# A hybrid decoder trunk on one core: gates by tanh, statistics over more steps, one convolution tile on GpSimd, prologue and tail in another order

## The chip, the core and the metric

The kernel runs on one core of a Trainium2 chip. The time is the device time of one execution, in microseconds, of a single program that holds the whole computation. PE is TensorE, ACT is ScalarE, DVE is VectorE, POOL is GpSimd, SP is SyncE, which here only issues DMAs. Each engine has its own instruction queue and works it off in order; engines wait for each other by semaphores.

## The reference

Two layers over 512 tokens of width 1024, in float32. Each layer:

```python
h = h + 0.5 * swiglu(rms(h), ffn1_wi, ffn1_wo)             # width 2816
n = rms(h);  z = n @ w_in                                  # conv, sgu, q, kv, 24 head gates, 3 x 1024 gates
y_a = silu(layer_norm(causal_depthwise_conv31(a * sigmoid(g)) + bias)) @ conv_out
y_b = (u * (tril(ws) @ v + b)) @ sgu_out                   # u, v = gelu(z_sgu), v normed, chunks of 128
y_c = nsa(rms(q), kv, sigmoid(z_ngate)) @ nsa_out          # compressed, selected and window attention, 8 heads
g_a, g_b, g_c = split(sigmoid(z_merge), 3)
h = h + (g_a * y_a + g_b * y_b + g_c * y_c) @ w_out
h = h + cross_attention(rms(h), rms(mem))                  # 4 heads, 256 memory tokens
h = h + 0.5 * swiglu(rms(h), ffn2_wi, ffn2_wo)
```

With 512 tokens, all eight blocks of 64 are selected, so the selected and the window attention have the same mask.

## The kernel before

**Weights.** Activations lie transposed, features on partitions and 512 tokens in the free dimension. Every product is made of *units*: a tile of up to 1024 x 128 weights against 512 tokens. For precision, weight and activation are split in a high and a low part and three products are added (high x high, high x low, low x high; PE, lines 600, 603, 606), so a unit of 8 row blocks is 24 matmuls and one of 4 is 12. A unit's path: SP loads it into one of two `raw` slots (`unit`, it waits for the low half of the unit two before); ACT copies it to `wH` (`split`, line 1110, called three units ahead by `ahead`); POOL subtracts to `wL` (`low`, line 569); PE multiplies into one of four PSUM banks `pg`; DVE takes the result out (`evac`).

**The attention stage.** Four pairs of heads times four query tiles give 16 steps s; step s has `COLS[s % 4] + 1` key tiles (4, 1, 3 and 2 of them). Before it lies the opening: the units of the last two query pairs (`U_QP2`) and the first two gates, with the spatial gating's transposes and products dropped between their matmuls (`opening`, one piece every four matmuls). Then for i = 1 to 16 PE runs `branch(i - 1)` (12 matmuls) and `gate(i + 1)` (24), with a piece of `attention(i, p)` after every second matmul: p = 0, 3, 6, ... transposes a group of step i-1's probabilities into the one bank `pT` (`turned`, line 651), p = 1 and 7 compute the scores of step i (line 808), p = 5, 8, ... multiply by the values (line 860). ACT's queue in step i is: `split`, `turned_out(i-1, 0)`, `exps(i, 0)`, `turned_out(i-1, 1)`, `split`, `turned_out(i-1, 2)`, `exps(i, 1)`, the other `turned_out`, `weighted(i)`, `merge_gate(i)` (line 1248). DVE's is `maxes(i, 0)` (line 1787), evacuation of the gate unit, `maxes(i, 1)`, of the branch unit, `weigh(i)` (lines 1800, 1805). `exps` waits for `maxes`, `weigh` for `exps`, `weighted` for `weigh`, the next `turned` for `weighted`.

**What lies beside it on DVE.** The convolution: 4 tiles of 31 taps (`conv(count)`, line 1631), done in portions from the conv units on; up to two running tiles are held in PSUM, in the attention all are in SBUF. `conv(count)` takes taps in turn from the first two unfinished tiles. Its LayerNorm needs a mean and a variance, summed over partitions by PE with a matrix of ones (`middle`, line 867). Query pairs are normalised by `squares`, `stat` on PE, `root` on ACT (line 1153) and a reciprocal on DVE (`normed`, lines 1494 and 1607). The order of the groups and statistics that pass `pT` is the list `order`, and each has its place in it (`STEP`).

**The rest.** The prologue loads x, transposes it on PE, loads 19 small parameter arrays and four of convolution weights, transposes them and copies them to `pall`; each layer copies its part to `par` (line 1587). `norm` makes high and low parts of the scaled input (lines 1110 and 1501). The two layers are passes of one loop on every engine. In the cross-attention, `xo_part(k)` (lines 1069 to 1071) accumulates four output units head by head beside the chain of the last head.

## Time and profile before

| | us |
|---|---|
| median of 3 runs | 2892.61 (2889.74 to 2893.19) |
| the profiled execution's own time | 2888.34 |
| its span | 2886.6 |
| PE busy | 2735.6 (95%) |
| DVE, ACT, POOL busy | 1210.4, 1194.8, 1149.1 |
| mean granted clock of TensorE | 0.974 |

The profile gives, for each engine, busy time, groups of instructions by line and shape, what ended each idle time, and the share of full speed that TensorE's clock was granted. Lines are those of the kernel before; line 1110 is the copy that all ACT copies go through. Weight loads (PEld) overlap PE.

### The profile page before, as it was taken

To read this page: it belongs to the slowest core of one execution; us is meant where nothing else is said; L and a number is where in the kernel's file an instruction comes from. 1 tells how busy PE (TensorE), PEld (TensorE's weight loads), DVE (VectorE), ACT (ScalarE), POOL (GpSimd) and SP (SyncE) were. 2 spreads that over 40 slices of the span, in tenths; PEclk is the share of its full clock that TensorE was granted. 3 is DMA by queue.
4 is the path that set the end of the run, shared out by engine and by line. 5 is a ranking of instruction groups with operands and counts; after the bars stand their busy time and mean duration, and the time that the engine had idled before them with its cause. 6 is when DMAs were issued, how large, how long until landed. Compare 5 with 4: busy or idle time off the path is not lost.

```text
span 2886.6 us, 39881 instructions
## 1 busy us (share of the span) xinstructions
PE 2735.6 (95%) x13132; PEld 2155.3 (75%) x13132; DVE 1210.4 (42%) x1860; ACT 1194.8 (41%) x1758; POOL 1149.1 (40%) x502
## 2 busy tenths in 40 slices
PE   6999999987999989999999999999889999899999
PEld 5888888754567867888878888886556687688887
DVE  4222267677334444121241212776863354431212
ACT  4322343455774454222252223334566644542321
POOL 3443453322325514444444444433223363244443
PEclk8999999988999999999999999999889999999999
DMA  3335333211114313333333352422112242133332
GB/s 103 105 95 124 103 103 81 66 45 41 45 48 117 106 41 102 95 96 101 88 89 102 95 132 87 106 74 59 44 34 56 70 115 83 52 102 95 96 101 80
DMA packets 493309, 243.61 MB, mean 84 GB/s; under 512 B 49656, under 2 KB 491362, under 8 KB 493154
## 3 DMA queue, kind: packets, MB, share of 16 engines
q1 hardware_dynamic: 493154, 241.62, 30.1%
q8 instruction: 88, 1.44, 0.2%
q14 instruction: 67, 0.55, 0.1%
HBM read 239.46 MB, written 2.10 MB: 84 GB/s over the span
## 4 chain that ended last, share of the span: by engine, by line
issue 61%; POOL 26%; PE 12%; POOLq 1%; DVE 0%; DVEq 0%
POOL wL L569 26%; PE pg L600 4%; PE pg L606 4%; PE pg L603 4%; POOLq L568 1%; POOLq L574 1%; DVE big L2050 0%; DVE xT L1538 0%; PE pg L651 0%; DVEq L72 0%; POOL tab L553 0%; POOL tab L535 0%; POOL sacc L534 0%; POOLq L561 0%; POOL tabc L555 0%
## 5 line engine op out<-in xcount | busy, mean ns | idle before, releaser
L569 POOL TENSOR_TENSOR wL<-raw,wH 128x1024 fp32r<-128x1024 f32 (+1 forms) x480 | 1144.8, 2386 | 1714.5 <-ACT wH L1110 1714.4
L600 PE MATMUL pg<-gxH,wH 128*128 128x512 f32 (+1 forms) x2448 | 974.8, 398 | 32.3 <-DVE gxL L1501 25.8
L606 PE MATMUL pg<-gxH,wL 128*128 128x512 f32 (+1 forms) x2448 | 956.9, 391 | 0.0
L603 PE MATMUL pg<-gxL,wH 128*128 128x512 f32 (+1 forms) x2448 | 953.0, 389 | 0.0
L1110 ACT ACTIVATE wH<-raw 128x1024 fp32r<-128x1024 f32 (+1 forms) x480 | 475.5, 991 | 564.7 <-PE pg L606 376.5
L600 PEld LDWEIGHTS pg<-gxH,wH 128*128 128x128 f32 x2448 | 466.1, 190 | 150.0 <-issue 33.7
L603 PEld LDWEIGHTS pg<-gxL,wH 128*128 128x128 f32 x2448 | 466.0, 190 | 105.5 <-issue 20.1
L606 PEld LDWEIGHTS pg<-gxH,wL 128*128 128x128 f32 x2448 | 466.5, 191 | 92.1 <-issue 3.0
L606 PE MATMUL pg<-hH,wL 128*128 128x512 f32 x1024 | 410.9, 401 | 0.0
L600 PE MATMUL pg<-hH,wH 128*128 128x512 f32 x1024 | 406.9, 397 | 3.7 <-POOL wL L569 3.7
L603 PE MATMUL pg<-hL,wH 128*128 128x512 f32 x1024 | 406.1, 397 | 0.0
L1538 DVE SCALAR_TENSOR_TENSOR xT<-pg,xT 128x512 f32<-128x512 f32 x128 | 88.4, 691 | 421.3 <-PE pg L606 419.2
L603 PEld LDWEIGHTS pg<-hL,wH 128*128 128x128 f32 x1024 | 194.4, 190 | 53.2 <-issue 13.3
L600 PEld LDWEIGHTS pg<-hH,wH 128*128 128x128 f32 x1024 | 194.9, 190 | 44.9 <-POOL wL L569 4.5
L606 PEld LDWEIGHTS pg<-hH,wL 128*128 128x128 f32 x1024 | 195.2, 191 | 38.0 <-issue 1.0
L1110 ACT ACTIVATE hH<-tmp 128x512 f32 x88 | 55.6, 632 | 302.5 <-DVE tmp L1553 302.5
L1553 DVE TENSOR_TENSOR tmp<-pg,tmp 128x512 f32<-128x512 f32 x88 | 60.9, 692 | 255.1 <-PE pg L606 252.7
L1548 DVE TENSOR_TENSOR tb<-pg,rstd 128x512 f32<-128x512 f32 x88 | 60.8, 690 | 246.6 <-PE pg L606 245.2
L1164 ACT ACTIVATE tmp<-tb 128x512 f32<-128x512 f32 x88 | 55.6, 632 | 258.5 <-DVE tb L1548 258.4
L1263 ACT ACTIVATE prob<-prob,nb 128x512 f32<-128x512 f32 (+3 forms) x128 | 70.9, 554 | 106.1 <-DVE nb L1790 105.8
L1631 DVE SCALAR_TENSOR_TENSOR convb<-convb,par 128x512 f32<-128x512 f32 x110 | 110.4, 1028 | 4.4
L651 PE MATMUL pA<-ident,prob 128*128 128x128 f32 x416 | 66.5, 287 | 46.0 <-ACT sq L1110 32.6
(218 smaller groups left out, 2085.9 us busy)
## 6 DMA issues: line engine op xcount, KB each, us to landing
raw<-in_ffn_wi SPq DMA_DIRECT2D x352, 256.0 KB, 3.1
raw<-in_w_in SPq DMA_DIRECT2D x200, 256.0 KB, 3.2
raw<-in_ffn_wo SPq DMA_DIRECT2D x128, 256.0 KB, 3.0
raw<-in_ffn_wo SPq DMA_DIRECT2D x64, 192.0 KB, 2.6
raw<-in_xkv SPq DMA_DIRECT2D x32, 256.0 KB, 3.1
raw<-in_w_out SPq DMA_DIRECT2D x32, 256.0 KB, 3.1
raw<-in_sgu_out SPq DMA_DIRECT2D x32, 128.0 KB, 2.2
raw<-in_conv_out SPq DMA_DIRECT2D x32, 128.0 KB, 2.2
```

The source lines that it names most:

```text
L569: pool.tensor_tensor(wL[:, s % 4, 0:n, :], raw[:, s % 2, 0:n, :], wH[:, s % 4, 0:n, :].bitcast(F32), ALU.subtract)\
L600: mm(o, wH[:, s, k, :], rh(k), start=(k == 0), stop=False)
L603: mm(o, wH[:, s, k, :], rl(k), start=False, stop=False)
L606: last = mm(o, wL[:, s, k, :], rh(k), start=False, stop=(k == kt - 1))
L651: return pe.transpose(dst, src, ident[0:k, 0:k])
L1110: return act.activation(o, i, ACT.Copy, **kw)
L1164: act.activation(sil, tb[:, 0, :], ACT.Silu).then_inc(silu, 1)
L1263: act.activation(t, t, ACT.Exp, bias=nb[:, s % 2, b, e:e + 1], scale=-1.0, accum_out=dn[:, s % 2, b, e:e + 1])
L1538: STT(xT[:, k, :], bank, by, xT[:, k, :], ALU.mult, ALU.add).then_inc(evac, 1)
L1548: TTt(tb[:, 0, :], bank, rstd[:, :], ALU.mult).then_inc(evac, 1)
L1553: TTt(hb, bank, sr, ALU.mult).then_inc(evac, 1)
L1631: STT(to, cin[:, j, k:k + T], w, o, ALU.mult, ALU.add)
```

## The change

Sigmoids of gates are written as (1 + tanh(x/2)) / 2: the merge gates' half goes into the residual's factor of W_out (0.5 for 1.0), the branch product becomes (tanh + 1) x bank in one instruction, and the head gates are scaled when they are copied. The convolution's own sigmoid stays. The roots of query pairs 2 and 3 move from the opening into steps 2 and 3, through `pT`; the mean from step 6 to step 5; the variance stays in step 7. Convolution tile 0 goes to POOL, one tap behind each `low` from U_KV + 2 on and two from U_QP2 on; DVE waits for it (`conv_in`) ahead of the mean's sum. DVE's portions in the attention become 3 in step 2, 3 and 3 in step 3 and all the rest at the end of step 4. The high and low copies of the convolution's output are spread over step 8. Two of the memory's low halves come before the last branch. `xo_part` covers three units, and its first part comes before the last head's norms and scores. In the prologue ACT issues 19 parameter loads, and the third weight split follows the first norm's high halves, which wait only for their own residual; the next layer's `par` is copied ahead of the second FFN.

```diff
@@ the order of turned groups and statistics
+EXTRA = {2: "q2", 3: "q3", 5: "mean"}
-if i == 6:
-    order.append("mean")
+if i in EXTRA:
+    order.append(EXTRA[i])
@@ SP: the loads of gains and norms (11 + 8 DMAs) leave; act.dma_start issues them ahead of act.wait_ge(consts, 1)
-for g, at in ((norm_ffn1, G_F1), (norm_mix, G_MIX), (norm_xattn, G_X),
...
-        sp.dma_start(ctab[at:at + n, 0:L, cols], g).then_inc(pro_par, 16)
@@ GpSimd
             low(l, first + s, i)
 with pool.Fori(0, L) as l:
-    lows(l, 0, U_XKV)
+    lows(l, 0, U_KV)
+    k, o, term = 0, cacc[:, CT, :], wsn[:, :, :].rearrange("p g t -> p (g t)")
+    for u in range(U_KV, U_XKV):
+        if u == U_KV + 2:
+            pool.wait_ge(cin_in, risen(cin_in, l, 1))
+        low(l, u)
+        for _ in range(0 if u < U_KV + 2 else 1 if u < U_QP2 else 2):
+            if k == CONV_W:
+                break
+            w = col(P_CW + CT * CONV_W + k)
+            if k == 0:
+                pool.tensor_scalar(o, cin[:, CT, 0:T], w, col(P_CB + CT), ALU.mult,
+                                   ALU.add)
+            else:
+                pool.tensor_scalar(term, cin[:, CT, k:k + T], w, 0.0, ALU.mult,
+                                   ALU.add)
+                pool.drain()
+                pool.tensor_tensor(o, o, term, ALU.add)
+            pool.drain()
+            k += 1
+            if k == CONV_W:
+                pool.drain().then_inc(conv_in, 1)
+    assert k == CONV_W
     lows(l, U_XKV, U_XO)
     for u in range(U_XO, U_F2):
@@ PE: middle, opening, attention
         pe.wait_ge(stat_in, risen(stat_in, l, s))
-        mm(bank[:, :], ones[:, :], sacc[:, :], start=True, stop=True).then_inc(st_mm, 1)
+        weights = bdon if key in ("q2", "q3") else ones
+        mm(bank[:, :], weights[:, :], sacc[:, :], start=True, stop=True)\
+            .then_inc(st_mm, 1)
...
             v_turned((0, 3, 6, 10).index(p))
-        if p in (5, 9, 14, 16):
-            mixed((5, 9, 14, 16).index(p))
+        if p in (5, 9, 12, 15):
+            mixed((5, 9, 12, 15).index(p))
         if p == 1:
...
             scores((0, 0))
-        if p == 11:
-            pe.wait_ge(sg_out, risen(sg_out, l, 2))
-            stat(l, 8, bdon)
         if p == 13:
             scores((0, 1))
-        if p == 19:
-            pe.wait_ge(sg_out, risen(sg_out, l, TT))
-            stat(l, 9, bdon)
     def attention(i, p):
-                middle("mean", 10)
+            elif i in EXTRA and a == n:
+                middle(EXTRA[i], {"q2": 8, "q3": 9, "mean": 10}[EXTRA[i]])
         elif p % 3 == 1:
@@ PE: cross-attention
-        for m in range(4):
+        for m in range(3):
...
+    xo_part(0)
     x_norms(3)
     x_scores(3)
-    xo_part(0)
     x_turned(2, 0)
...
     xo_part(3)
-    for m in range(4, 8):
+    for m in range(3, 8):
@@ ACT: norm and the start of a layer
     def high(k):
-        act.wait_ge(evac, risen(evac, l, 0 if u0 is None else u0 + k + 1))
+        act.wait_ge(evac, risen(evac, l, k + 1 - KD if u0 is None else u0 + k + 1))
         copy(dst(k), xT[:, k, :], scale=col(gain + k)).then_inc(gx_h, 1)
...
             high(k)
+        split(l, 2)
     for k in range(KD):
         if u0 is not None:
...
+    split(l, 0)
+    split(l, 1)
     made[0] = 3
     act.wait_ge(par_in, risen(par_in, l, 1))
     norm(l, 0, G_F1, gx_tile, None)
@@ ACT: gates
     act.wait_ge(ng_in, risen(ng_in, l, 1))
-    act.activation(hb, sr, ACT.Sigmoid).then_inc(ng_sig, 1)
+    act.activation(hb, sr, ACT.Tanh, scale=0.5).then_inc(ng_sig, 1)
...
         act.wait_ge(evac, risen(evac, l, gate_unit(n) + 1))
-        act.activation(t, t, ACT.Sigmoid).then_inc(mg_sig, 1)
+        act.activation(t, t, ACT.Tanh, scale=0.5).then_inc(mg_sig, 1)
@@ ACT: opening and steps
+    def conv_high(k):
+        copy(hH[:, BR["A"] + k, :], cacc[:, k, :]).then_inc(br_h, 1)
     ahead(l, U_QP2)
...
     v_out(3)
-    root(l, 8, rv, 1.0 / DH)
     ahead(l, gate_unit(0))
...
     weighted(0)
-    root(l, 9, rv, 1.0 / DH)
     merge_gate(0)
...
         turned_out(i - 1, 0)
+        if i == 8:
+            conv_high(0)
         if i < NS:
...
         turned_out(i - 1, 1)
-        if i == 6:
-            act.wait_ge(st_mm, risen(st_mm, l, STEP["mean"] + 1))
-            copy(sil, pT, scale=-1.0 / DC).then_inc(st_out, 1)
+        if i == 8:
+            conv_high(1)
         ahead(l, gate_unit(i + 1))
...
             exps(i, 1)
+        if i == 8:
+            conv_high(2)
         for g in range(3, n):
             turned_out(i - 1, g)
+        if i in (2, 3):
+            act.wait_ge(st_mm, risen(st_mm, l, STEP[EXTRA[i]] + 1))
+            act.activation(rv[:, :], pT, ACT.Sqrt, bias=eps[:, 0:1],
+                           scale=1.0 / DH).then_inc(st_out, 1)
+        if i == 5:
+            act.wait_ge(st_mm, risen(st_mm, l, STEP["mean"] + 1))
+            copy(sil, pT, scale=-1.0 / DC).then_inc(st_out, 1)
         if i < NS:
             weighted(i)
         merge_gate(i)
             act.drain()
-            for k in range(KB):
-                copy(hH[:, BR["A"] + k, :], cacc[:, k, :]).then_inc(br_h, 1)
+        if i == 8:
+            conv_high(3)
     def merged_high(m):
@@ DVE: parameters
-with dve.Fori(0, L) as l:
-    dve.tensor_copy(par[:, :], pall[:, bass.ds(l, 1), :]
+def par_of(n):
+    dve.tensor_copy(par[:, :], pall[:, bass.ds(n, 1), :]
                     .rearrange("p a c -> p (a c)")).then_inc(par_in, 1)
...
        ALU.mult)
+dve.memset(pall[:, L, :], 0.0)
+dve.drain()
+par_of(0)
+dve.drain().then_inc(evac, risen(evac, 0, 0))
+dve.sem_inc(sq_used, risen(sq_used, 0, 0))
+with dve.Fori(0, L) as l:
     norm(l, 0, gx_high, gx_low, G_F1, None)
     root_of(l, 0, rstd)
@@ DVE: taps, branches
         TTt(cin[:, j, CONV_W - 1:TP], tb[:, 0, :], sil, ALU.mult)
-        dve.drain()
-        inputs.append(j)
+        if j == CT:
+            dve.drain().then_inc(cin_in, 1)
+        else:
+            dve.drain()
+            inputs.append(j)
     dve.memset(cin[:, :, 0:CONV_W - 1], 0.0)
     for j in range(4):
...
         dve.wait_ge(mg_sig, risen(mg_sig, l, n + 1))
+        t = mrg[:, m, :] if n < 8 else (hb, sr)[n % 2]
+        bank = ready(l, u)
+        STT(t, tb[:, n % 2, :], 1.0, bank, ALU.add, ALU.mult).then_inc(evac, 1)
         if n < 8:
-            scaled(mrg[:, m, :], l, u, by=tb[:, n % 2, :])
             return
-        t = (hb, sr)[n % 2]
-        scaled(t, l, u, by=tb[:, n % 2, :])
         dve.drain()
         last = TTt(mrg[:, m, :], mrg[:, m, :], t, ALU.add)
@@ DVE: opening and steps
     dve.wait_ge(ng_tr, risen(ng_tr, l, 1))
-    dve.tensor_copy(gates[:, :, :], pT[:, :].rearrange("p (a c) -> p a c", a=4)
-                    [:, :, 0:NG])
+    TS(gates[:, :, :], pT[:, :].rearrange("p (a c) -> p a c", a=4)[:, :, 0:NG], 0.5,
+       0.5, ALU.mult, ALU.add)
     dve.drain()
...
     scaled(qT[:, 2, :], l, U_QP2)
-    squares(qT[:, 2, :])
     maxes(0, 0)
     mixed(1)
-    normed(l, 8, qT[:, 2, :], g8[:, 2:3])
-    dve.drain().then_inc(q_ok, 1)
     scaled(qT[:, 3, :], l, U_QP2 + 1)
-    squares(qT[:, 3, :])
+    mixed(2)
     maxes(0, 1)
-    mixed(2)
     mixed(3)
...
     weigh_c(0)
-    normed(l, 9, qT[:, 3, :], g8[:, 3:4])
-    dve.drain().then_inc(q_ok, 1)
-    conv(4)
+    def late_pair(j):
+        dve.wait_ge(st_out, risen(st_out, l, STEP[f"q{j}"] + 1))
+        dve.reciprocal(rv[:, :], rv[:, :])
+        dve.drain()
+        STT(qT[:, j, :], qT[:, j, :], g8[:, j:j + 1], rv[:, :], ALU.mult, ALU.mult)
+        dve.drain().then_inc(q_ok, 1)
     for i in range(1, NS + 1):
...
         gate(i)
-        if i < 6:
-            conv(5)
+        if i in (2, 3):
+            conv(3)
         if i == 7:
...
         if i == 8:
-            low("A", 4)
+            low("A", 4, (0,))
         if i < NS:
             maxes(i, 1)
+        if i == 8:
+            low("A", 4, (1,))
         branch(i - 1)
+        if i == 8:
+            low("A", 4, (2,))
         if i < NS:
...
                 maxes_c(i // TT + 1)
-        if i < 5:
-            conv(5)
-        if i == 5:
+        if i == 8:
+            low("A", 4, (3,))
+        if i == 1:
+            squares(qT[:, 2, :])
+        if i == 2:
+            late_pair(2)
+            squares(qT[:, 3, :])
+        if i == 3:
+            late_pair(3)
+            conv(3)
+        if i == 4:
             conv(KB * CONV_W)
+            dve.wait_ge(conv_in, risen(conv_in, l, 1))
             TTt(sacc[:, :], cacc[:, 0, :], cacc[:, 1, :], ALU.add)
...
             stat_given(None)
-        if i == 6:
+        if i == 5:
             dve.wait_ge(st_out, risen(st_out, l, STEP["mean"] + 1))
             for k in range(KB):
                 TTt(cacc[:, k, :], cacc[:, k, :], sil, ALU.add)
             dve.drain()
+        if i == 6:
             for k in range(KB):
                 TTt(sacc[:, :] if k == 0 else hb, cacc[:, k, :], cacc[:, k, :],
@@ DVE: end of the branches, residual of W_out, second FFN
             gate(NS + 1 + m)
+        if m == 7:
+            memory_low(0)
+            memory_low(1)
         branch(NS + m)
         if m == 4:
...
             last.then_inc(mem_sc, 1)
-    for i in range(4):
+    for i in range(2, 4):
...
     norm(l, 2, lambda k: xnorm_tile(hH, gxH, k), lambda k: xnorm_tile(hL, gxL, k), G_X,
-         residual(l, U_WO, 1.0))
+         residual(l, U_WO, 0.5))
...
     norm(l, 3, gx_high, gx_low, G_F2, residual(l, U_XO, 1.0))
     root_of(l, 15, rstd)
+    par_of(l + 1)
     ffn(l, U_F2, 1, None)
     dve.drain()
```

## Rows read from the trace of the kernel before

**Rows 1.** Page, part 1: busy time, share of the span, instructions of each engine.
```profile
PE 2735.6 (95%) x13132; PEld 2155.3 (75%) x13132; DVE 1210.4 (42%) x1860; ACT 1194.8 (41%) x1758; POOL 1149.1 (40%) x502
```

**Rows 2.** Waits of PE, whole span: who ended them, us in total, times, longest.
```profile
PE pA L651 <- ACT sq L1110: 45.1, 32, 5.0
...
PE pg L600 <- DVE gxL L1930: 5.6, 2, 2.8
```

**Rows 3.** Stretches of layer 0's attention: length, busy of each engine, clock, DMA.
```profile
551.00:598.20 47.20, 37.95 (x189) 27.89 (x187) 31.54 (x44) 26.88 (x40) 11.88 (x5) 0.96 0.19 51
598.20:619.00 20.80, 15.38 (x83) 9.81 (x84) 18.28 (x30) 10.19 (x23) 5.07 (x2) 0.75 0.15 39
619.00:672.30 53.30, 46.61 (x252) 29.80 (x253) 43.81 (x81) 33.21 (x64) 14.75 (x6) 0.97 0.17 45
672.30:688.10 15.80, 13.69 (x87) 8.61 (x86) 14.36 (x24) 10.82 (x24) 5.19 (x2) 1.00 0.18 52
688.10:709.00 20.90, 17.51 (x64) 10.33 (x64) 12.87 (x26) 10.96 (x20) 4.78 (x2) 0.76 0.15 38
709.00:732.90 23.90, 18.93 (x102) 11.97 (x100) 15.59 (x28) 12.71 (x24) 5.68 (x2) 0.86 0.13 34
732.90:755.40 22.50, 18.90 (x94) 11.87 (x93) 7.72 (x22) 18.54 (x32) 4.89 (x2) 0.92 0.13 35
755.40:875.00 119.60, 114.40 (x646) 75.19 (x645) 37.98 (x121) 82.17 (x158) 38.76 (x17) 0.99 0.20 54
```

**Rows 4.** Groups by line and shape: count, busy us, mean ns, idle before them.
```profile
L1248 ACT ACT_TABLE_LOAD x34 | 43.6, 1283 | 0.6
...
L1631 DVE SCALAR_TENSOR_TENSOR convb<-convb,par 128x512 f32<-128x512 f32 x110 | 110.4, 1028 | 4.4
...
L569 POOL TENSOR_TENSOR wL<-raw,wH 128x512 fp32r<-128x512 f32 x16 | 21.6, 1348 | 119.8 <-ACT wH L1110 119.8
L553 POOL TENSOR_SCALAR_AFFINE_SELECT tab<-tab 128x512 f32<-128x512 f32 x1 | 0.6, 612 | 0.0
```

**Rows 5.** Timeline of DVE and POOL, end of step 5: start, length, instruction.
```profile
683.56 5.71 DVE L1631 SCALAR_TENSOR_TENSOR convb<-convb,par 128x512 f32<-128x512 f32 x7
689.35 2.71 DVE L1899 TENSOR_TENSOR sacc<-convb 128x512 f32<-128x512 f32 x1
...
689.10 2.41 POOL L569 TENSOR_TENSOR wL<-raw,wH 128x1024 fp32r<-128x1024 f32 x1 [8.25 <-ACT wH L1110]
```

**Rows 6.** Timeline of DVE, PE and ACT, from step 4 to step 5.
```profile
667.56 0.16 DVE L1805 TENSOR_TENSOR wv<-wv,gates 128x4 f32<-128x4 f32 x1
...
674.50 0.65 PE L651 MATMUL pA<-ident,prob 128*128 128x128 f32 x4 [1.46 <-ACT sq L1110]
675.76 0.40 ACT L1263 ACTIVATE prob<-prob,nb 128x128 f32<-128x128 f32 x1
...
676.85 0.60 ACT L1110 ACTIVATE sq<-pA 128x512 f32<-128x512 f32 x1 [0.22 <-PE pA L860]
```

**Rows 7.** Timeline of POOL in the key/value units, one of seven like it.
```profile
442.26 2.40 POOL L569 TENSOR_TENSOR wL<-raw,wH 128x1024 fp32r<-128x1024 f32 x1 [3.05 <-ACT wH L1110]
```

**Rows 8.** Timeline of PE in the prologue.
```profile
8.63 6.23 PE L651 MATMUL pg<-ident,big 128*128 128x128 f32 x32 [8.63 <-DMA big<-in_x]
...
18.05 1.09 PE L651 MATMUL pA<-ident,convb 126*128 126x126 f32 x4 [3.19 <-DMA convb<-in_conv_w]
...
32.50 0.79 PE L600 MATMUL pg<-gxH,wH 128*128 128x512 f32 x1 [13.36 <-DVE gxL L1501]
```

**Rows 9.** Timeline of DVE and PE between the layers.
```profile
1453.93 0.54 DVE L1587 COPY par<-pall 128x250 f32 x1 [3.11 <-issue]
...
1456.14 0.80 PE L600 MATMUL pg<-gxH,wH 128*128 128x512 f32 x1 [6.05 <-DVE gxL L1501]
```

**Rows 10.** Timeline of PE in layer 0's cross-attention.
```profile
1045.08 3.46 PE L1019 MATMUL pA<-kT,qT 128*128 128x256 f32 x8 [3.11 <-ACTq L1428]
...
1071.70 0.57 PE L600 MATMUL pg<-hH,wH 128*128 128x512 f32 x1 [1.84 <-POOL wL L569]
```

More of the change, by code:

```diff
@@ L247, in mm_index @@
         def mm_index(n):
-            return n if n < 10 else {12: 10, 13: 11, 15: 12}[n]
+            return n if n < 8 else {12: 8, 13: 9, 15: 10}[n]
         rises = {}
@@ L272, in trunk @@
         stat_in = sig("stat_in", NSTAT - 1)
-        stat_mm = sig("stat_mm", 13)
-        stat_rt = sig("stat_rt", 13)
+        stat_mm = sig("stat_mm", 11)
+        stat_rt = sig("stat_rt", 11)
         silu = sig("silu", 2 * FT)
@@ L292, in trunk @@
         conv_sig = sig("conv_sig", 4)
+        cin_in = sig("cin_in", 1)
+        conv_in = sig("conv_in", 1)
         gelu = sig("gelu", 8)
@@ L354, in trunk @@
         BR = {"B": 4, "A": 0, "C": 4}
+        CT = 0
         BRANCH = (1, 0, 2)
@@ L911, in attention @@
                             turned(i - 1, g)
-                        elif i == 6 and a == n:
-                            middle("mean", 10)
+                        elif i in EXTRA and a == n:
+                            middle(EXTRA[i], {"q2": 8, "q3": 9, "mean": 10}[EXTRA[i]])
                     elif p % 3 == 1:
@@ L1177, in ffn @@
                     u += KD
+            for g, at in ((norm_ffn1, G_F1), (norm_mix, G_MIX), (norm_xattn, G_X),
+                          (mem_norm, G_MEM), (norm_ffn2, G_F2), (conv_b, P_CB),
+                          (conv_ln_g, P_LG), (conv_ln_b, P_LB), (sgu_norm, P_SG),
+                          (xq_norm, P_XQ), (xk_norm, P_XK)):
+                n = g.shape[1] // P
+                act.dma_start(ctab[at:at + n, 0:L, :], g.rearrange("l (a b) -> a l b", b=P))\
+                  .then_inc(pro_par, 16)
+            for half in range(2):
+                cols = slice(half * DH, (half + 1) * DH)
+                for g, at in ((nsa_q_norm.rearrange("l (a c) -> a l c", a=1), P_NQ),
+                              (nsa_k_norm.rearrange("l a c -> a l c"), P_NK),
+                              (cmp_pe.rearrange("l i a c -> i a l c")[0], P_PE),
+                              (cmp_pe.rearrange("l i a c -> i a l c")[1], P_PE + CMP_LEN)):
+                    n = g.shape[0]
+                    act.dma_start(ctab[at:at + n, 0:L, cols], g).then_inc(pro_par, 16)
             act.wait_ge(consts, 1)
             with act.Fori(0, L) as l:
-                for u in range(3):
-                    split(l, u)
+                split(l, 0)
+                split(l, 1)
                 made[0] = 3
@@ L1822, in branch, with low @@
                         last.then_inc(m_in, 1)
-                def low(name, first):
+                def low(name, first, part=range(KB)):
                     src = uG if name == "B" else cacc
-                    for k in range(KB):
+                    for k in part:
                         dve.wait_ge(br_h, risen(br_h, l, first + k + 1))
```

22 lines of the change are left out of this document (2 added, 20 removed).

## The prediction, made blind

> **What bounds the kernel now.** The page comes first: PE is busy 95% of the span, no other engine above 42% [rows 1]. An edit gains only what it takes from PE's 151 us of idle time, or from stretches in which PE works at a lowered clock. The waits of PE say whose idle time it is [rows 2]: 45.1 us end with an ACT copy of transposed probabilities, 5.6 with the memory's low halves; the rest is single waits, shown below. Then the stretches: I cut the attention of layer 0 at the gate activations of its steps [rows 3]. Opening and 16 steps take 324 us, of which PE idles 40.6: 9.3 in the opening, 5.4 in step 1, 6.7 in steps 2 to 4, 2.1, 3.4, 5.0 and 3.6 in steps 5 to 8, 5.2 in steps 9 to 16. In the same rows the granted clock is below 1: length times what is missing from 1 gives 20 us, some 18 of them with PE at work (the levels are 2.4 and 1.2 GHz, and the low rows are those with long stalls). So 59 us per layer are to be had. DVE is busy 31.5 of 47.2 and 18.3 of 20.8 us at the start, 38.0 of 119.6 at the end: the early steps wait for DVE and its convolution taps, the late ones for ACT.
>
> **Table loads (tanh).** Exponentials and sigmoids alternate: a load of 1283 ns stands before 34 of the 48 gates [rows 4]. Following the functions through the code I count 39 loads per layer from `exps_c(0)` to the memory's root; 10 stay (roots of q2, q3, var and memory, the Silu, each with its return). 29 x 1.283 = 37 us less for ACT per layer. ACT is no bound; it counts where it ends PE's idle time. A step loses two loads, 2.57 us, more than PE idles in most of steps 9 to 16 (5.2 us in eight steps): I leave 0.8. In step 8 four high copies are spread as well: 3.6 becomes 0.3. No row shows Tanh; that it stands beside Exp without a load is my assumption, as Copy does beside both; bounds are 0 and 2 loads per step (rival 3). The Trainium skill (ScalarE: Activation LUTs, "Table sets: the hidden batching unit") lists tanh in the exponential's set, and in the sigmoid's too; by the first the sum is as I take it, by the second it is rival 3.
>
> **Convolution taps.** I walked the taps through the code. Before: 68 ahead of the attention, 56 in it (4, then 5 and 5 per step, 12 in step 5, then three additions). After, tile 0 is GpSimd's; DVE does 60 ahead and 33 in it: none in step 1, 3 in step 2, 6 in step 3, and **24 at one go at the end of step 4**, the three additions behind them. At 1028 ns in the mean [rows 4] DVE loses 23 x 1.03 = 24 us per layer. In line, seven take 5.71, 0.816 each. An addition that began at 689.35 ended only 0.55 after GpSimd's operation of 2.41 us had: it was held 2.2 us [rows 5].
> *The block.* DVE's weights of step 4 are done at 667.7 [rows 6]. From there 24 x 0.816 = 19.6, two holds 4.4, additions 2.3 and another hold: 27.5 us, with bounds of 22 without holds and 33 with five, in which DVE serves nobody. Queued behind is `maxes(5, 0)`; ACT's in-order queue has `exps(5, 0)` before `turned_out(4, 1)`, and PE's third group of transpositions in step 5 needs that. PE starts the second group at 674.50; without the load before the gate it is 673.3; two pieces later, at 676, it stands. After the block come the maxima (0.6) and what is 1.7 from the exponentials' start to the copy's end [rows 6], say 2.5: 667.7 + 27.5 + 2.5 = 697.7. Stall 21.7; I take 22 in place of 2.1 (bounds 15 and 28).
> *The rest of the spreading.* Step 1 has no taps and no root ahead of its gate: 5.4 becomes 1.5. Steps 2 and 3 get a root with its load on ACT ahead of `weighted`, for which PE's next group waits, and a reciprocal on DVE behind `weigh`, for which the next maxima wait, but fewer taps: 6.7 becomes 7.2. The opening loses both reciprocals and roots (9.3 becomes 4) and gains GpSimd's taps beside it (7). Step 6: the mean was asked for a step earlier, 3.4 becomes 0.5. Step 7: four additions leave the work ahead of `var`, 5.0 becomes 2. Sum: 7 + 1.5 + 7.2 + 22 + 0.5 + 2 + 0.3 + 0.8 = 41.3 against 40.6: **idle time in the attention stays the same.**
> *Clock.* 18 us of slow work in stretches 1, 2, 3 and 5 to 8 of [rows 3]. After: one long stall, whose slow time lies mostly inside it (3.5 of work), a short one in step 7, two or three before: 9.4. Gain 8.6. **Net 8 per layer**, bounds -6 and +16.
>
> **GpSimd's tile.** 31 taps, each a tensor_scalar and a tensor_tensor of 128x512 with drains. The second kind is 1348 ns; the first is not in the trace: its bounds are the select of the same size (612) and again 1348 [rows 4]. It reads one tensor, as the select: I take 0.8, and with two drains 2.4 a tap (2.1 to 3.2). Its cover: 16 taps stand one behind each low half, where GpSimd idles 3.05 between operations of 2.40 [rows 7]; from 3.0 up PE's three units of lead absorb it. 15 come two per unit: 2.4 + 1.35 + 4 x 2.4 = 13.4 us per gate-and-branch pair, against steps of 15 or more. They end in step 2 or 3, so DVE's new wait for them at the end of step 4, with the additions queued behind it, costs nothing; it would from a tap of 5. The other price is DVE's: an operation with two SBUF inputs can be held by a tap's parts, 0.7 on average; 3 us in the opening, 2 in steps 1 and 2, both in the numbers above. The Trainium skill (GPSIMD Engine Reference, "8. Key points") speaks against this edit: DVE is about twice as fast elementwise, and the two contend when DVE has two SBUF inputs. The trace agrees on the second with its held addition of 2.71 us.
>
> **Prologue.** PE's x transposes end at 14.9, but the parameters' wait to 18.05 for 23 small loads, and the first product starts at 32.50 after 13.36 idle [rows 8], since the weights' loads follow all of them and ACT splits three units first. Now ACT issues 19 of the loads, the weights follow x and four loads on SP, and the third split comes after the high halves. Parameters turned by 16.0, four copies at 0.54 or less 2, then the 2.2 that copy, high and low half take from 1453.93 to 1456.14 [rows 9]: 20.3. **Gain 12** (9 to 13).
> **Between the layers** PE idles 6.05 [rows 9]. High halves can now run under the last residuals, and the parameter copy moved ahead of the FFN (1 us on DVE there, beside four filled banks). But DVE shows 3.11 of "issue" before its first operation of the pass: that stays. Of the 2.2 the copy and the high half go: **1.4** (0.5 to 5).
> **Cross-attention.** PE waits 3.11 for exponentials and later 1.84 for a weight [rows 10]. Nine products (PE's pace is 5.45 us a unit of 24 [rows 7], so 2.05) now fill the first wait; head 3's chain starts earlier as `xo_part(0)` is out of its middle; the fourth unit covers the weight. DVE's last norm starts as much earlier. **5.5 per layer** (2 to 7).
> **Memory.** The 5.6 us are 2.8 per layer; two low halves before the last branch take them away, and some slow time: **3 per layer** (2 to 4). (1 + tanh) x bank and the factor 0.5 replace operations of the same size: 0.
>
> **Sum.** 2 x 8 + 12 + 1.4 + 2 x 5.5 + 2 x 3 = 46. The profiled execution took 2888.3 (span 2886.6); the three runs 2889.7 to 2893.2, so I add 2: 2888.3 - 46 + 2 = **2844**. Own range 2820 to 2878.
>
> **Rivals.** (1) *The block is hidden*: the stall is 8, 14 us per layer less, 2816. For it: before, 7 taps and the additions, 10 us in step 5, cost only 3.4 in step 6. Against: this block is near three times as long, behind in-order queues. Chance 0.16.
> (2) *Slower: DVE held by GpSimd.* From the key/value units to step 2 DVE issues some 35 operations with two SBUF inputs per layer (squares, normalising products, mixes, low halves, weights). If each is held for 1.35, DVE gets 47 us more; what passes its idle time lands on PE. It decides at 23 us per layer, where it eats the gain; at 35 it gives 2890 + 2 x 12 = 2914. For it: the held addition. Against: DVE idles 15.7 us in the opening alone [rows 3]. Chance 0.12.
> (3) *Tanh still switches*: 8 us idle and 2 of slow work per layer come back, 2864. Chance 0.05.
> (4) Nothing measurable: the stall at 28 and the small parts at their low ends, 2889. Chance 0.07. The forecast has 0.60.
> A difference of 0.2% (6 us) is about what a measurement can tell from none. Faster 0.60 + 0.16 + 0.05 and a part of (4), 0.83; same 0.06; slower 0.11. The range 2805 to 2890 leaves out rival 2 and the far end of rival 1.
>
> **What would show it.** Right: few loads before gates; 22 to 24 taps in a row on DVE and, in step 5, a PE stall of 15 to 28 us that ends with an ACT copy, twice; first product near 20.5; `var`'s wait near 2. Wrong: no such stall (1); DVE operations of 1.5 to 2.7 us all over the opening and PE waiting for DVE before step 4 (2); a load before each gate (3); DVE waiting for GpSimd at the end of step 4 (a tap above 5).

## The result, and the profile after

The change makes the kernel faster by a little under 1%: 2865.37 us (median of 4 runs, 2862.85 to 2866.07) against 2891.18 for the kernel before on the same chip (2889.66 to 2893.19), ratio 0.9915, 95% interval 0.9903 to 0.9928. The medians are 26 us apart; the forecast had 46. The profiled execution took 2862.85 (span 2861.1).

The page's line of busy times and the waits of PE, of the kernel after (waited for: us in total, times, longest us):

```profile
PE 2710.0 (95%) x13132; PEld 2138.5 (75%) x13132; DVE 1167.4 (41%) x1802; ACT 1115.8 (39%) x1700; POOL 1229.9 (43%) x624
...
PE pA L663 <- ACT sq L1115: 66.5, 18, 18.3
PE pg L612 <- DVE gxL L1533: 18.7, 7, 6.3
PE pA L663 <- ACT prob L1115: 12.2, 12, 2.3
PE pA L877 <- DVEq L1521: 9.6, 2, 4.8
PE pA L627 <- DVEq L1521: 9.2, 6, 2.5
...
PE pg L612 <- POOL wL L558: 4.4, 6, 1.7
...
PE pg L612 <- DVE gxL L1984: 2.3, 2, 1.1
```

The table loads before merge gates and before the exponentials, of the kernel after:

```profile
L1269 ACT ACT_TABLE_LOAD x6 | 7.7, 1283 | 0.1
...
L1284 ACT ACT_TABLE_LOAD x2 | 2.6, 1283 | 0.0
```

Against [rows 1, 2]: PE's busy time fell by 25.6 us with the same 13132 matmuls; its idle time is 151 us in both kernels. The mean granted clock rose from 0.974 to 0.979. An estimate from these (span times what is missing from 1, 75 us before and 60 after) gives 15 us; what the other 10 are is open. The wait for ACT's copies of probabilities has grown from 45.1 to 66.5 us, and two of its 18 pieces, one in each layer, are 18.3 and 18.2 us long.

The stretches of layer 0's attention, cut as in [rows 3] (length; busy us and instructions of PE, weight loads, DVE, ACT, POOL; granted clock, DMA share, GB/s):

```profile
544.30:585.70 41.40, 35.43 (x183) 27.37 (x182) 26.38 (x38) 19.08 (x33) 37.71 (x29) 0.92 0.22 58
585.70:598.30 12.60, 11.86 (x79) 7.96 (x78) 4.56 (x17) 7.58 (x21) 8.85 (x7) 1.00 0.25 65
598.30:653.10 54.80, 48.67 (x253) 29.79 (x253) 33.15 (x69) 31.77 (x63) 11.38 (x6) 0.94 0.16 44
653.10:690.20 37.10, 18.83 (x106) 12.19 (x104) 23.41 (x40) 8.68 (x23) 4.10 (x2) 0.72 0.08 22
690.20:702.40 12.20, 12.19 (x60) 7.67 (x58) 7.12 (x20) 7.65 (x19) 3.67 (x2) 1.00 0.24 64
702.40:724.60 22.20, 17.42 (x97) 11.20 (x98) 15.76 (x27) 11.16 (x22) 3.92 (x2) 0.85 0.14 36
724.60:747.50 22.90, 18.06 (x88) 10.22 (x86) 8.58 (x21) 16.60 (x31) 3.64 (x2) 0.93 0.13 35
```

Length less PE's busy time is 6.0 us of idle time in the opening, 0.7 in step 1, 6.1 in steps 2 to 4, **18.3 in step 5**, 0 in step 6, 4.8 in step 7, 4.8 in step 8 (and 1.7 in steps 9 to 16, not shown). Step 5 on the three engines:

```profile
649.85 21.56 DVE L1668 SCALAR_TENSOR_TENSOR convb<-convb,par 128x512 f32<-128x512 f32 x24
671.49 0.69 DVE L1952 TENSOR_TENSOR sacc<-convb 128x512 f32<-128x512 f32 x1
672.25 1.46 DVE L1955 TENSOR_TENSOR sacc<-sacc,convb 128x512 f32<-128x512 f32 x2
674.07 0.06 DVE L1827 MEMSET nb<- 128x2 f32 x1 [0.36 <-issue]
...
674.79 0.40 ACT L1284 ACTIVATE prob<-prob,nb 128x128 f32<-128x128 f32 x1 [19.56 <-DVE nb L1830]
...
675.88 0.60 ACT L1115 ACTIVATE sq<-pA 128x512 f32<-128x512 f32 x1 [0.22 <-issue]
...
676.53 1.12 PE L663 MATMUL pA<-ident,prob 128*128 128x128 f32 x4 [18.27 <-ACT sq L1115]
...
2092.78 1.11 PE L663 MATMUL pA<-ident,prob 128*128 128x128 f32 x4 [18.20 <-ACT sq L1115]
```

It is the chain that the prediction drew: 24 taps, three additions, then the maxima; ACT's exponentials waited 19.56 us for them with the copy of the transposed group queued behind; PE stood 18.27 us for that copy. The last line is the same wait in layer 1. DVE did not wait for GpSimd's last tap: its first addition follows the taps at once.

**Where the gain arose.** The starts of DVE's reciprocals are landmarks that both kernels share. The *lead* is how much earlier the kernel after reaches such a point than the kernel before, in us, worked out from their start times:

| landmark | layer 0 | layer 1 |
|---|---|---|
| first FFN's statistic, mix's statistic | 8.4 | 15.7 |
| start of the attention's opening | 6.7 | 14.3 |
| memory's keys (first statistic) | 14.4 | 21.6 |
| memory's keys (second statistic) | 13.0 | 20.1 |
| second FFN's statistic | 15.6 | 25.6 |

A word for what follows: DVE or GpSimd is *held* when an operation on SBUF tensors of one of them takes longer, ending only after an operation of the other has ended; the extra time is a *hold*.

### The profile page after: what moved, and what is told of

Read it like the earlier page. It is cut to its first block, busy times and chain, and to the rows that moved or that the text cites. A ratio compares the mean times of both kernels' runs of the same rounds, so it can differ in the third digit from the quotient of the medians.

```text
span 2861.1 us, 39635 instructions
## 1 busy us (share of the span) xinstructions
PE 2710.0 (95%) x13132; PEld 2138.5 (75%) x13132; DVE 1167.4 (41%) x1802; ACT 1115.8 (39%) x1700; POOL 1229.9 (43%) x624
## 4 chain that ended last, share of the span: by engine, by line
issue 45%; PE 27%; POOL 20%; POOLq 6%; DVE 0%; DVEq 0%; DMA 0%; ACT 0%; SPq 0%; ACTq 0%
POOL wL L558 19%; PE pg L612 9%; PE pg L615 9%; PE pg L618 9%; POOLq L585 3%; POOLq L587 3%; POOL wsn L583 1%; POOLq L557 0%; POOLq L563 0%; DVE big L2108 0%; DVEq L1538 0%; DMA raw<-in_w_in 0%; DVE gxL L1533 0%; ACT wH L1115 0%; PE pA L627 0%
## 5 line engine op out<-in xcount | busy, mean ns | idle before, releaser
L558 POOL TENSOR_TENSOR wL<-raw,wH 128x1024 fp32r<-128x1024 f32 (+1 forms) x480 | 1089.1, 2270 | 1596.3 <-ACT wH L1115 1592.2
L612 PEld LDWEIGHTS pg<-gxH,wH 128*128 128x128 f32 x2448 | 462.8, 189 | 142.8 <-issue 31.5
L663 PEld LDWEIGHTS pA<-ident,prob 128*128 128x128 f32 x416 | 50.3, 144 | 83.8 <-ACT sq L1115 49.3
```

What stands on the lines that cost most here:

```text
L558: pool.tensor_tensor(wL[:, s % 4, 0:n, :], raw[:, s % 2, 0:n, :], wH[:, s % 4, 0:n, :].bitcast(F32), ALU.subtract)\
L612: mm(o, wH[:, s, k, :], rh(k), start=(k == 0), stop=False)
L663: return pe.transpose(dst, src, ident[0:k, 0:k])
```

## The experiments

Each was run beside the kernel before on the same chip: the first four together, the next four together, then two and two. The kernel before had medians of 2888.4 to 2891.2, so differences between experiments are taken from their ratios, times 2890. For the kernel after the two medians alone give 0.9911 where its ratio is 0.9915, so a difference against it can be 1.3 us smaller than stated.

| kernel | median us | ratio, 95% interval |
|---|---|---|
| after | 2865.37 | 0.9915 [0.9903, 0.9928] |
| e1_tanh | 2871.07 | 0.9936 [0.9923, 0.9949] |
| e2_prologue | 2888.45 | 0.9993 [0.9984, 1.0002] |
| e3_cross | 2883.29 | 0.9976 [0.9966, 0.9986] |
| e4_spread | 2845.49 | 0.9847 [0.9835, 0.9860] |
| e5_no_taps | 2829.41 | 0.9797 [0.9783, 0.9810] |
| e6_dve_tile | 2874.27 | 0.9956 [0.9943, 0.9970] |
| e7_arranged | 2835.75 | 0.9820 [0.9806, 0.9833] |
| e8_no_prologue | 2855.66 | 0.9889 [0.9874, 0.9904] |
| e9_two_left | 2834.69 | 0.9809 [0.9796, 0.9823] |
| e10_late_taps | 2824.25 | 0.9774 [0.9761, 0.9788] |
| e11_after_late_taps | 2858.91 | 0.9887 [0.9871, 0.9902] |
| e12_sgu_taps | 2823.16 | 0.9768 [0.9755, 0.9781] |

Layer 0 step by step, lengths in us between the activations of merge gates ("opening": from the reciprocal of the second query pair to the first gate):

| | opening | 1 | 2 | 3 | 4 | 5 | 6 | 7 | 8 |
|---|---|---|---|---|---|---|---|---|---|
| before | 42.7 | 20.9 | 17.3 | 15.5 | 20.5 | 15.8 | 20.9 | 23.9 | 22.5 |
| after | 36.9 | 12.6 | 18.2 | 15.6 | 21.0 | 37.2 | 12.1 | 22.2 | 22.9 |
| e4_spread | 36.9 | 14.6 | 19.8 | 22.4 | 21.8 | 16.8 | 12.1 | 22.0 | 21.8 |
| e5_no_taps | 32.7 | 13.1 | 18.3 | 23.2 | 22.0 | 16.8 | 12.1 | 22.2 | 23.3 |
| e6_dve_tile | 33.0 | 15.7 | 22.9 | 25.9 | 26.8 | 22.9 | 12.1 | 23.3 | 21.8 |
| e7_arranged | 37.3 | 16.5 | 20.4 | 17.4 | 19.3 | 23.4 | 12.2 | 15.9 | 22.5 |
| e9_two_left | 36.5 | 17.1 | 22.2 | 18.2 | 20.1 | 17.8 | 12.2 | 15.9 | 21.9 |
| e10_late_taps | 33.3 | 16.7 | 21.9 | 18.2 | 20.1 | 16.5 | 12.2 | 15.9 | 22.7 |

The opening and eight steps take 199.9 us before and 198.7 after: the stall of step 5 eats nearly all that the others gain.

### One part at a time

**e1_tanh**, the gates and what goes with them, on the kernel before:

```diff
-                act.activation(hb, sr, ACT.Sigmoid).then_inc(ng_sig, 1)
+                act.activation(hb, sr, ACT.Tanh, scale=0.5).then_inc(ng_sig, 1)
-                    act.activation(t, t, ACT.Sigmoid).then_inc(mg_sig, 1)
+                    act.activation(t, t, ACT.Tanh, scale=0.5).then_inc(mg_sig, 1)
```

> The kernel before with the gates by tanh alone (and the branches, the small gates and the residual's factor that go with it). Theory: 28 of the 34 loads before gates go; PE loses some 5 us of idle time per layer in steps 1 to 16 (5.2 in steps 9 to 16 become 1 to 2, step 8's 3.6 little) and 2 to 3 us of work at a lowered clock, so the time is 2891 - 16 = 2875. Rival A, ACT is no bound and its loads lie beside PE's work nearly everywhere: 2886 to 2891. Rival B, tanh needs a load of its own: 34 loads stay and nothing moves.

Measured: 18 us, 16 expected. In its trace the loads before merge gates number 4; in the kernel after they are 6 where they were 34 [rows 4], and ahead of the exponentials (line 1284) 2 are left. Rivals A and B fall. The two layers differ: by the reciprocals' start times the lead over the kernel before grows by 4.6 us through layer 0 and by 14.5 through layer 1, so the same edit need not be worth the same at two places. The Trainium skill (ScalarE: Activation LUTs, "Table sets: the hidden batching unit") has tanh in the exponential's set; the trace agrees by those counts.

**e2_prologue**, the prologue and the layer's start, on the kernel before:

```diff
-                sp.dma_start(ctab[at:at + n, 0:L, :], g.rearrange("l (a b) -> a l b", b=P))\
+                act.dma_start(ctab[at:at + n, 0:L, :], g.rearrange("l (a b) -> a l b", b=P))\
...
-                for u in range(3):
-                    split(l, u)
+                split(l, 0)
+                split(l, 1)
...
+                par_of(l + 1)
                 ffn(l, U_F2, 1, None)
```

> The kernel before with the prologue and the layer's start alone (19 loads issued by ACT, third split behind the high halves, high halves bound to their residual only, parameters copied ahead of the FFN). Theory from the two traces: the first product stands at 22.4, two thirds of the forecast's gain of 12 reach the end (8.4) and the junction gives under 1: 2891 - 9 = 2882, and the lead of 8.4 over the kernel before is the same 8.4 when layer 0's attention starts. Rival A, the forecast's terms 12 + 1.4: 2878. Rival B, the lead is lost again in the key and value units as in the kernel after (6.7 left at the opening of the attention): the loss there belongs to the prologue and not to GpSimd's taps, 2885.

Measured: 2888.45, no difference. All expected times missed. The lead of 8.4 is whole at the opening, as the theory had it (so rival B falls: the loss there in the kernel after is not the prologue's), but it is gone later: 6.2 and 4.1 at the memory's two statistics, 2.2 at the second FFN, and nothing at the end of layer 1. Where it goes shows beside the memory's units. DVE and POOL, before (first three lines) and e2_prologue (last four):

```profile
909.27 0.69 DVE L1820 TENSOR_TENSOR big<-big,tmp 128x512 f32<-128x512 f32 x1
909.88 4.69 DVE L1922 TENSOR_TENSOR hL<-big,hH 128x512 fp32r<-128x512 f32 x4
...
909.94 2.88 POOL L569 TENSOR_TENSOR wL<-raw,wH 128x1024 fp32r<-128x1024 f32 x1 [0.59 <-ACT wH L1110]
```

```profile
901.76 2.06 DVE L1826 TENSOR_TENSOR big<-big,tmp 128x512 f32<-128x512 f32 x1
903.75 6.88 DVE L1928 TENSOR_TENSOR hL<-big,hH 128x512 fp32r<-128x512 f32 x4
...
900.87 2.40 POOL L554 TENSOR_TENSOR wL<-raw,wH 128x1024 fp32r<-128x1024 f32 x1 [4.31 <-ACT wH L1095]
903.86 2.82 POOL L554 TENSOR_TENSOR wL<-raw,wH 128x1024 fp32r<-128x1024 f32 x1 [0.58 <-ACT wH L1095]
```

The same operations on two SBUF tensors meet POOL's low halves at another moment: 0.69 becomes 2.06, ending 0.55 after the low half, and 4.69 becomes 6.88. PE then waits longest 4.4 for the memory's low halves, in place of 2.8.

**e8_no_prologue**, the same part taken out of e4_spread (below):

> The spread version with the prologue and the layer's start of the kernel before (23 loads on SP, three splits first, parameter copy at the layer's start). In e2_prologue the prologue's lead of 8.4 was eaten between step 7 and the memory's units. Theory (the gain is 8.5 us and its loss in e2_prologue was the work of chance meetings of GpSimd's low halves with DVE's additions, which fall out otherwise here): 2845 + 6 to 10 = 2853. Rival A, a lead of the prologue is always eaten further on: 2843 to 2848. Rival B, the junction's part counts too: 2858 or more.

Measured: 12 us more than e4_spread, above the expected 6 to 10; its lag is 8.2 at the start and 10.0 to 10.9 from the memory's units on. So the part is worth 12 here and 2 there (interval of that run: nothing to 5). Rival A falls; of rival B's junction the trace shows 0.4. The gain at the start is the same; what differs is how much of it is lost or added to further on. That this is by chance meetings of GpSimd's low halves with DVE's operations fits both pairs of traces but is not shown: no run shifted the low halves alone.

**e3_cross**, on the kernel before:

```diff
+                xo_part(0)
                 x_norms(3)
                 x_scores(3)
-                xo_part(0)
...
-                    for m in range(4):
+                    for m in range(3):
```

> The kernel before with the order of the cross-attention's end alone (xo_part(0) first, three units in parts in place of four). Theory from the two traces: 2.5 us per layer, 2891 - 5 = 2886. Rival A, the forecast's 5.5 per layer: 2880. Rival B, nothing, since the exponentials' wait is only moved: 2891.

Measured: 7 us (4 to 10); the interval holds the theory's 5 and not the forecast's 11. In the trace the lead grows by 0.4 us in layer 0's cross-attention and by 3.3 in layer 1's. The wait for exponentials fell from 9.2 to 5.0 us over the two layers, the weight's wait did not change (longest 1.84 before, 1.8 here), and one for the last head's normalised probabilities grew from 2.8 to 4.1.

### The block of 24 taps

**e4_spread**, on the kernel after:

```diff
-                    if i in (2, 3):
-                        conv(3)
+                    if i < 5:
+                        conv(4)
                     if i == 7:
...
                     if i == 1:
                         squares(qT[:, 2, :])
+                        conv(5)
                     if i == 2:
                         late_pair(2)
                         squares(qT[:, 3, :])
+                        conv(4)
                     if i == 3:
                         late_pair(3)
-                        conv(3)
+                        conv(4)
```

> The kernel after with the 33 taps that DVE does in steps 1 to 5 spread as 4 + 5, 4 + 4, 4 + 4, 4 + 4 in place of 0, 3, 6 and 24 at one go. Theory (the block causes the stall): the wait of 18.3 us in step 5 is gone in both layers, steps 1 to 5 idle some 14 us in all in place of 25, slow work shrinks by 3: 14 to 18 us per layer, 2865 - 32 = 2833. Rival A, DVE's taps cost PE their time wherever they stand, the stall is only dealt out to the steps: 2855 to 2865. Rival B, the wait of 18 us hangs on something else in step 5 (the wait for GpSimd's last tap, the statistic of the mean) and stays: 2865.

Measured: 20 us less than after, so the block did cause the stall; rival B falls. But the gain is under two thirds of the expected 32: step 5 gives back 20.4, steps 3 and 4 take 7.6, steps 1 and 2 3.6. Rival A is half right. Step 3, its first line DVE, then PE:

```profile
621.40 5.20 DVE L1668 SCALAR_TENSOR_TENSOR convb<-convb,par 128x512 f32<-128x512 f32 x4
...
629.83 1.12 PE L663 MATMUL pA<-ident,prob 128*128 128x128 f32 x4 [5.32 <-ACT sq L1115]
```

Four taps stand behind a late pair and its squares, ahead of the next maxima, and take 1.3 us each, with a low half of POOL beside them from 621.20 to 623.57. The mean of such taps is 819 ns in the kernel after, where most stand in a stall with POOL nearly idle, and 1022 ns here: beside PE at work they are held more often.

**e7_arranged**, on the kernel after, the squares of step 6 in two halves, and **e9_two_left** on it:

```diff
-                    if i in (2, 3):
-                        conv(3)
+                    if i < 5:
+                        conv(5 if i < 3 else 6)
+                    if i == 6:
+                        square_sum((0, 1))
                     if i == 7:
...
                     if i == 1:
                         squares(qT[:, 2, :])
+                        conv(5)
...
                         late_pair(3)
-                        conv(3)
...
                     if i == 6:
+                        square_sum((2, 3))
                         stat_given(None)
```

```diff
-                        conv(5 if i < 3 else 6)
+                        conv(6 if i < 3 else 7)
```

> The kernel after with the 33 taps placed behind the first gate of a step (5, 5, 6, 6) and only 5 and 6 at the ends of steps 1 and 4, none behind the late pairs of steps 2 and 3, and half of the squares for var moved ahead in step 6. Theory (what stands on DVE between the end of one step and the next step's maxima is what PE waits for): the waits of 5.3 and 5.5 in steps 3 and 4 of the spread version shrink to 2, var's 4.8 to 2.5: 7 to 9 us per layer less, 2829. Rival A, the total of DVE's work in a step decides and not its place: 2843 to 2847. Rival B, the middle of the step is the sensitive place, since the second maxima feed exp and weights: above 2850.

> The arranged version (e7_arranged) with the taps behind the first gate of steps 1 to 4 as 6, 6, 7, 7 in place of 5, 5, 6, 6, so that 2 and not 6 stand at the end of step 4 ahead of the additions. Theory (what stands ahead of the next maxima costs PE time, one for one once the cover is used up): four taps, 3.3 us, leave step 5's wait of 3.8, and steps 1 to 4 lose 1 to 2: 2836 - 4 = 2832. Rival A, DVE's total decides: 2836. Rival B, the additions, held by GpSimd, are what step 5 waits for, and the middle of the steps is full: above 2838.

Measured: e7 8 us less than e4_spread, half of the 14 to 18 that the theory had. e9 is 3 us less again for an expected 4, but the two intervals overlap. Steps 3 and 4 lose 5.0 and 2.5, step 7 loses 6.1 (`var`'s wait of 4.8 is 0.3, the halved squares did that); but step 5 gained 6.6 in e7, and of the 5.6 that e9 took from it 4.1 came back in steps 1 to 4. So the place matters where a statistic's work stands already, and once each step's *cover* (DVE time that PE does not wait for) is used up, taps only move their price.

### GpSimd's tile

**e5_no_taps** leaves the 31 taps of channel tile 0 out of e4_spread (a constant stands in the tile); **e6_dve_tile** gives them back to DVE (`CT = None`, 7 and 7 taps in steps 1 to 4).

> The spread version (e4_spread) with GpSimd's 31 taps left out, so that the convolution of channel tile 0 is not computed; everything else, DVE's 93 taps included, stays. Theory (the taps hold DVE's operations on two SBUF tensors and move GpSimd's low halves, at a small price): the 2 us per layer lost in the key and value units come back, and some 2 in the steps' taps: 2845 - 8 = 2837. Rival A, the second rival of the prediction, holds of some 23 us per layer: under 2805. Rival B, GpSimd's low halves hold DVE and its taps do not: 2845.

> The spread version with convolution tile 0 back on DVE: 124 taps there, 68 ahead of the attention as before, 56 as 7 + 7 in each of steps 1 to 4. Theory (DVE's taps ahead of the maxima cost PE its time in the early steps): three more taps at each of eight places, 2.5 us each, half of it stalls, and the opening gets holds back: 8 to 12 us per layer, 2861 to 2869. Rival A, the tile on GpSimd buys nothing, since DVE has the time: 2840 to 2848. Rival B, GpSimd's share slowed DVE by more than it took from it: under 2840.

Measured: without the taps 14.5 us less, with the tile on DVE 31.5 more. So moving the tile to GpSimd is worth 31.5 us in this arrangement, against an expected 16 to 24, and it still costs 14.5, near twice the expectation. Of that 2.0 per layer lie in the key and value units, as expected, and **4.2 in layer 0's opening and 5.1 in layer 1's** (in layer 0 the gain over e4_spread grows from 1.4 to 5.6 there), which was not. Layer 0 gives part of it back by the second FFN, where 3.7 are left. The opening of the kernel after:

```profile
548.18 0.70 POOL L583 TENSOR_SCALAR wsn<-convb,par 128x512 f32<-128x512 f32 x1
549.03 1.26 POOL L586 TENSOR_TENSOR convb<-convb,wsn 128x512 f32<-128x512 f32 x1
550.46 0.69 POOL L583 TENSOR_SCALAR wsn<-convb,par 128x512 f32<-128x512 f32 x1 [0.17 <-issue]
551.30 1.26 POOL L586 TENSOR_TENSOR convb<-convb,wsn 128x512 f32<-128x512 f32 x1
552.77 2.56 POOL L558 TENSOR_TENSOR wL<-raw,wH 128x1024 fp32r<-128x1024 f32 x1 [0.20 <-issue]
...
560.07 2.40 POOL L558 TENSOR_TENSOR wL<-raw,wH 128x1024 fp32r<-128x1024 f32 x1 [0.20 <-issue]
...
552.24 1.06 ACT L1115 ACTIVATE wH<-raw 128x1024 fp32r<-128x1024 f32 x1 [2.16 <-DMA raw<-in_w_in]
...
553.84 1.11 PE L663 MATMUL pA<-ident,big 128*128 128x128 f32 x4 [4.99 <-ACT sq L1115]
```

GpSimd no longer waits for ACT (`<-issue`): it runs back to back, one low half and two taps in 7.3 us (552.77 to 560.07), while units of 24 matmuls come every 5.45. It falls behind; a `raw` slot comes free only with its low half, so the load is late, ACT's split waits 2.16 us for it, and queued behind the split on ACT is the copy that PE's transposes wait 4.99 us for. Without the taps that wait is 2.8:

```profile
PE pA L655 <- ACT sq L1107: 2.8, 1, 2.8
```

Beside this, an addition of the spatial gate takes 2.47 at 560.55 and four low halves of the branch 4.70; the kernel without the taps has 0.91 and 2.50. How the 4.2 us divide between late loads and held DVE operations no run tells.

**e10_late_taps** on e9_two_left and **e11_after_late_taps** on the kernel after, the same line, one tap per unit up to the first branch:

```diff
-                    for _ in range(0 if u < U_KV + 2 else 1 if u < U_QP2 else 2):
+                    for _ in range(0 if u < U_KV + 2 else 1 if u < U_G + 2 else 2):
```

> The version before it (e9_two_left) with one GpSimd tap per unit up to the first branch and two only from there, so that the opening has four taps fewer beside it and steps 1 to 3 more. Theory (in the version without taps the opening was 5 us shorter per layer, held mixes and low halves): the opening gets back 1 to 2.5 us per layer, steps 2 and 3 lose under 1: 2829 if e9 gives 2832. Rival A, the holds only move with the taps: no difference to e9. Rival B, the last tap now comes late and DVE waits for it at the end of step 4: 5 us or more above e9.

> The kernel after with nothing changed but GpSimd's schedule: one tap per unit up to the first branch, two from there (as e10_late_taps against e9_two_left, where it gave 10 us). DVE's block of 24 taps stays. Theory (the two taps per unit beside the opening cost the changed kernel 3 to 4 us per layer there, whatever follows): 2865 - 8 = 2857. Rival A, the block hides it, since step 5's wait starts from DVE's queue and not from PE's: 2863 to 2866. Rival B, GpSimd's later taps now meet steps 1 to 3, which before had none: above 2866.

Measured: 10 us for e10, where 3 were expected, and 8 for e11 as expected (6.5 by the medians; its profiled run is 4 us below that of the kernel after, which was the fastest of four). The opening as cut above, of after and of e11_after_late_taps:

```profile
548.17:585.08 36.91, 30.94 (x151) 23.75 (x150) 25.72 (x36) 15.42 (x28) 33.43 (x28) 0.91 0.23 61
```

```profile
548.21:580.35 32.14, 28.59 (x147) 21.77 (x146) 24.10 (x36) 15.31 (x29) 28.50 (x22) 1.00 0.25 68
```

Six POOL operations fewer in it (28 to 22), 2.4 us less idle time of PE, and 2.3 us less of PE's own work, with the clock at 1.00 and not 0.91: 4.8 us from four taps moved by a few units. In e11 step 5 is 1.8 us longer than in the kernel after (39.0 for 37.2), so rival A, that the block hides it, is true of a part.

**e12_sgu_taps**, no taps beside the key and value units, one and two in turn beside the spatial gate's:

> The version with late taps (e10_late_taps) with none of GpSimd's taps beside the key and value units, twelve (one and two in turn) beside the eight units of the spatial gate, one per unit to the first branch, two from there. Theory (in the version without taps the key and value units were 2 us shorter per layer and the spatial gate's units no shorter): 2824 - 4 = 2820. Rival A, two taps in a unit of 5.45 us make GpSimd's low halves late and PE waits for them: above 2828. Rival B, no difference, 2822 to 2826.

Measured: 2823.16, 2 us less than e10_late_taps by ratio, inside the intervals: rival B, no difference. The trace has the expected 2.1 us at the key and value units of layer 0, and gives them back in steps 2 and 5 (23.1 and 17.8 for 21.9 and 16.5). These two are the fastest versions, 2.3% under the kernel before and 1.5% under the changed one.

## Why the prediction was right and wrong

The sign, the range and the main mechanism were right; the size was 20 us too large. By the leads at the landmarks the missing 20 us are: 3.6 in the prologue, 3.1 in the query, key and value units, 7.0 between the openings and the memory's first statistics, 2.8 between the memory's two statistics, 2.9 in layer 0's cross-attention, 1.2 between the layers. No single term is the cause.

- **Table loads**: 29 fewer per layer were counted, and the traces have 158 loads before and 100 after, 58 fewer in two layers; those before gates fell from 34 to 6. Alone the tanh is worth 18 us. Rival 3 falls.
- **The block**: forecast 22 (15 to 28), measured 18.3, ending with the copy that was named. The term that was too large is the holds: 24 taps and three additions took 23.9 (649.85 to 673.71) for 27.5, since three holds were added where PE, and with it POOL, stands still; only one low half of POOL (654.82, 2.82 us) fell into the block. (The sum was also added up short: its terms with three holds of 2.2 give 28.5.) Rival 1 falls.
- **Idle time of the attention**: forecast 41.3, measured 42.5. PE's busy time in it, the clock's term, fell by 8.1 (283.4 to 275.2) for 8.6, so the whole is 6.3 us shorter in layer 0 (324.0 to 317.7) for 8. But steps 7 and 8 are 4.8 and 4.8 for 2 and 0.3. In step 7 I counted four additions fewer ahead of `var` and let the wait go, while seven squares and additions still stood there; moving half of them (e7) took the wait to 0.3. In step 8 they are three waits for ACT's work, of 1.3, 1.8 and 1.8: tanh and the spread high copies did not take them away, and no run tests why. The opening's 6.0 for 7 hides the next point.
- **GpSimd's cover** is the step whose mechanism failed, though it is not what makes the 20 us: the opening's idle time came out as forecast. A tap was right (0.69 to 0.94 and 1.3, 2.3 with the gap, for 2.4). The taps ahead of the opening were put beside a pace of 5.45, the later ones beside "13.4 us per gate-and-branch pair" against steps of 15. The four units of the opening are no such pairs, each is a full unit: 2.4 + 2 x 2.3 and gaps is 7.3 against 5.45, and what absorbs it, three units of lead, was read as PE's when it hangs on two `raw` slots that POOL itself gives back. Taps in the opening cost 4.2 and 5.1 us there (e5), most of them avoidable by one line (e11).
- **Rival 2** (DVE held) is real in kind and wrong in size: 14.5 us for all of GpSimd's taps in the whole kernel, their lateness included, where the rival needed 23 per layer to eat the gain. The Trainium skill (SBUF — State Buffer, "SBUF: two separate sides") says that of a GpSimd operation and a DVE operation with two SBUF inputs the one that starts first has the shared ports for its whole instruction. The trace agrees both ways: GpSimd's 2.38 at 452.81 makes DVE's squares 2.75 at 452.98, and its tensor_scalar takes 3.95 at 447.21 beside two DVE additions of 128x992, ending 0.44 after the second.

```profile
452.81 2.38 POOL L558 TENSOR_TENSOR wL<-raw,wH 128x1024 fp32r<-128x1024 f32 x1 [0.20 <-issue]
...
452.98 2.75 DVE L1638 TENSOR_TENSOR sacc<-kT 128x512 f32<-128x512 f32 x1
...
447.21 3.95 POOL L583 TENSOR_SCALAR wsn<-convb,par 128x512 f32<-128x512 f32 x1
...
445.29 5.43 DVE L1712 TENSOR_TENSOR big<-prob,par 128x992 f32<-128x992 f32 x2
```

  The 1.4 to 1.7 us per layer lost between the mix's statistic and the opening were left out of the sum (holds stood in it only for the opening and for steps 1 and 2).
- **Prologue**: 12 forecast, 8.4 measured. The parameters were turned in time (PE's transposes end at 16.01), but the weights came at 16.97, and behind them a table load and two splits stand ahead of the high halves on ACT; then GpSimd's first low halves hold DVE's:

```profile
16.97 1.28 ACT L1115 ACT_TABLE_LOAD   x1 [16.97 <-DMA raw<-in_ffn_wi]
18.27 2.00 ACT L1115 ACTIVATE wH<-raw 128x1024 fp32r<-128x1024 f32 x2
20.18 5.00 ACT L1115 ACTIVATE gxH<-xT,par 128x512 fp32r<-128x512 f32 x8
...
20.91 10.27 DVE L1533 SCALAR_TENSOR_TENSOR gxL<-xT,par,gxH 128x512 fp32r<-128x512 f32 x8 [2.14 <-ACT gxH L1115]
...
19.40 5.13 POOL L558 TENSOR_TENSOR wL<-raw,wH 128x1024 fp32r<-128x1024 f32 x2 [13.87 <-ACT wH L1115]
```

  The first product stands at 22.36 for 20.3, and the next waits once more. The step left out is ACT's own queue.
- **Between the layers**: 1.4 forecast. PE idles 5.45 in place of 6.05 [rows 9]; the lead grows by 0.2. DVE's 3.16 of "issue" stayed as said; its first low half then took until 1440.06, 1.57 us in place of 0.80, with a low half of GpSimd from 1437.11 to 1439.45 beside it.
- **Cross-attention**: 5.5 per layer forecast, 2.6 and 5.5 measured. The exponentials' longest wait went from 3.11 to 1.5, but the 1.84 for the weight [rows 10] is 1.71: the fourth unit does not cover it.
- **Memory**: 3 per layer forecast. The waits for its low halves fell from 5.6 to 2.3 in all, but 1.3 and 1.5 of the lead were lost between the memory's two statistics; PE now waits for DVE's statistics (line 627: six waits, 9.2 us over the whole kernel, in place of one of 1.5). How much of that is holds and how much the shorter lead is open.
